# A two-block transformer kernel: the first block's layer norms, products and borders made token-major

## The chip, the cores and the metric

The kernel runs on one core of one Trainium2 chip. The metric is the device time of one execution in microseconds (us), the median of several. TensorE (PE) does the matrix products, VectorE (DVE), ScalarE (ACT) and GpSimd (POOL) the rest, and SyncE (SP) issues the weight loads.

## The reference, cut to what matters

Input `x` is 256 tokens of 1024 channels, float32. A first block of two layers and then a second block of two layers are computed. One layer of the first block is:

```python
y = _even_mixer(h, ...) if i == 0 else _odd_mixer(h, ...)        # both end in: @ w_out
h = _layer_norm(DN_ALPHA * h + y, ln1_g[i], ln1_b[i])
u = jnp.square(jax.nn.relu(h @ mlp_w1[i])) @ mlp_w2[i]           # 1024 -> 4096 -> 1024
h = _layer_norm(DN_ALPHA * h + u, ln2_g[i], ln2_b[i])
h = h + jax.nn.sigmoid(h @ ple_gate_w[i]) * (p[i] @ ple_w[i])    # p: 256 tokens x 256
```

`_layer_norm` takes mean and variance over the 1024 channels of a token. One layer of the second block is a gated feed-forward (1024 to 2816 and back), a mixer, and another gated feed-forward, with rms norms around each.

## The kernel before

All weights stream from HBM in units of 128 x 1024 floats (512 KB) through a ring of 12 slots. SP loads unit `n + 12` as soon as TensorE has handed slot `n` back (`k.freed`, a count, in order; the loop at lines 2587 to 2590). A unit is 8 blocks of 128 x 128. A float32 product of TensorE is recorded as two instructions, so a unit that is the stationary operand against all 256 tokens is 16 instructions of 256 columns.

**First block, feature-major.** An activation lies as 8 tiles of 128 channels x 256 tokens: `k.x` holds the residual and, after a norm, its result. `pe_columns` (L275 to L291) takes a unit as stationary blocks and the activation as the moving operand. `pe_unit` (L257 to L272) does the same for the down product. A layer norm sums over channels, which lie across partitions here, so `tail_tensor` (L2469) sums with products against a tile of ones: L2479 for the mean, L350 for the squares. `tail_vector.norm` (L2526) adds the residual (L2532), waits for the channel sums, subtracts the mean (L2537), takes the reciprocal of the deviation (L371) and scales (L2541). `tail_scalar.norm` squares (L359), takes the root (L364) and adds the bias (L2510). Each step needs the whole of the step before, and the next product needs the end of it. After the second norm come 8 units of gate product (L284 under `tail_tensor`), sigmoid (L2520), product with the embedding (L2549) and the sum with `k.x` (L2554). The embedding's 2 units are put beside the second norm (`embedded`, L2470). The output projections of both mixers are 8 units by `pe_columns` (L1869, L2289).

**Between the blocks.** `pe_square_sum` and `dve_rstd` make one feature-major rms norm. `turn_x` (L736) transposes the residual to token-major, and `turned_x` (L1132) copies it.

**Second block, token-major.** The residual `k.x_tok` is 2 tiles of 128 tokens x 1024 channels. A down or output product has 128 x 128 of the activation stationary and 512 columns of weight rows moving: 8 instructions of 512 columns for a unit (`pe_ffn_tok`, L458; `down`, L467). At a border the two token tiles are staggered. The last TAIL = 5 units are run for tile 0 first, `y_done` is counted, and they are run for tile 1 while ScalarE and VectorE norm tile 0 (`act_boundary`, L548; `dve_boundary`, L570). `pe_turn_h` (L399) transposes a normed tile into PSUM, 8 pieces of 128 x 128, and ScalarE and VectorE copy half each into `k.h`. `pe_lead` (L415) then runs the first units of the next product for tile 0 alone (128 columns an instruction, L425) and after that for tile 1 (L441), so that tile 1's norm has work beside it. The lead is LEAD = 3 hidden tiles of 2 units; the second tile's transposes stand ahead of the last unit of the first pass.

Each engine runs its own instructions in order; every `wait_ge` holds all that is behind it on that engine. The first block's mixers (`even_*`, `odd_*`) read `k.x`. Tables of sines and cosines for the odd mixer are made by `tables_vector` and `tables_scalar` (L2439, L2461) after the even mixer, on VectorE and ScalarE.

## Time and profile before

| | |
|---|---|
| median of 3 runs | 2330.22 us (2330.14 to 2334.64) |
| the profiled execution | 2334.19 us, its span 2332.3 us |
| TensorE busy | 2225.5 us, 95% |
| VectorE, ScalarE, GpSimd busy | 492.4, 342.0, 101.4 us |
| mean granted TensorE clock | 0.956 |
| HBM read | 296.98 MB, 128 GB/s over the span |
| chain that ended last | PE 92%, DVE 5%, ACT 1%, issue 1%, DVEq 1% |

The chain is followed back from the last instruction: what is on it sets the time. Busy time of an engine overlaps that of the others, and matmul ends are modelled, so two starts are a better measure of TensorE's work than its busy time. The granted clock is a share of full speed (2.4 GHz), and a stretch at 0.5 is 1.2 GHz.

### The profile page before, as it was taken

How to read it: one execution, taken by the hardware profiler on the slowest of the kernel's cores; microseconds unless marked ns; L12 is line 12 of the kernel's file. 1: busy time of each engine (PE TensorE's matmuls, PEld its weight loads, DVE VectorE, ACT ScalarE, POOL GpSimd, SP SyncE). 2: the span in 40 equal slices, each digit the busy share in tenths (PEclk: the TensorE clock that was granted, in tenths of full speed). 3: DMA queues.
4: the chain of work that ended last, by engine and by line, in shares of the span. 5: the costliest groups of instructions: out<-in, count | busy, mean ns of one | idle time of the engine just before them, and what ended most of it. 6: DMA issues, size and time to landing. Idle time of an engine off the chain costs nothing.

```text
span 2332.3 us, 26353 instructions
## 1 busy us (share of the span) xinstructions
PE 2225.5 (95%) x10308; PEld 1757.5 (75%) x10308; DVE 492.4 (21%) x1056; ACT 342.0 (15%) x773; POOL 101.4 (4%) x132
## 2 busy tenths in 40 slices
PE   8978899999878999999999999999999999999998
PEld 6755788888756788877777886877687778867776
DVE  0336310012452200021000463100110015530001
ACT  1113210001111100020000351100110013511001
POOL 0000000000000000000000070000000001600000
PEclk9965999999879999999999999999999999989999
DMA  6410244444202344434444421544464444124443
GB/s 256 149 37 0 73 145 153 153 135 134 93 35 67 114 153 153 150 130 129 151 153 143 148 71 57 178 153 153 145 218 153 153 149 140 63 68 158 153 153 117
DMA packets 81584, 299.47 MB, mean 128 GB/s; under 512 B 9120, under 2 KB 9248, under 8 KB 81248
## 3 DMA queue, kind: packets, MB, share of 16 engines
q1 hardware_dynamic: 80352, 293.87, 38.1%
q0 software_dynamic: 1152, 4.45, 0.5%
q8 instruction: 60, 0.98, 0.2%
q14 instruction: 20, 0.16, 0.0%
HBM read 296.98 MB, written 1.05 MB: 128 GB/s over the span
## 4 chain that ended last, share of the span: by engine, by line
PE 92%; DVE 5%; ACT 1%; issue 1%; DVEq 1%; DMA 0%; ACTq 0%; SPq 0%
PE psum L284 46%; PE psum L469 12%; PE psum L266 10%; PE psum L724 7%; PE psum L1674 5%; PE psum L2161 3%; PE psum L441 2%; PE psum L425 2%; PE psum L1558 1%; PE psum L2479 1%; PE psum L350 1%; PE psum L1622 1%; PE psum L404 0%; DVE sq L578 0%; DVE x L582 0%
## 5 line engine op out<-in xcount | busy, mean ns | idle before, releaser
L284 PE MATMUL psum<-h,ring 128*128 128x256 f32 x2976 | 654.7, 379 | 0.0
L284 PEld LDWEIGHTS psum<-h,ring 128*128 128x128 f32 x2976 | 565.1, 190 | 105.7 <-issue 32.5
L284 PE MATMUL psum<-x,ring 128*128 128x256 f32 x1728 | 391.4, 384 | 17.9 <-ACT x L2510 7.1
L284 PEld LDWEIGHTS psum<-x,ring 128*128 128x128 f32 x1728 | 332.8, 193 | 66.5 <-issue 16.3
L266 PE MATMUL psum<-hid,ring 128*128 128x256 f32 x1024 | 231.1, 379 | 0.0
L266 PEld LDWEIGHTS psum<-hid,ring 128*128 128x128 f32 x1024 | 194.6, 190 | 26.5
L469 PE MATMUL psum<-ring,hid 128*128 128x512 f32 x448 | 201.4, 592 | 0.0
L523 ACT ACTIVATE hid_act<-psum 128x256 f32<-128x256 f32 x88 | 33.8, 384 | 783.1 <-PE psum L284 729.0
L469 PEld LDWEIGHTS psum<-ring,hid 128*128 128x128 f32 x448 | 85.1, 190 | 83.2 <-issue 80.4
L538 DVE TENSOR_TENSOR hid<-psum,hid_act 128x256 f32<-128x256 f32 x56 | 23.8, 425 | 568.8 <-ACT hid_act L523 568.8
L469 PE MATMUL psum<-ring,space 128*128 128x512 f32 x256 | 112.3, 592 | 0.0
L339 DVE TENSOR_TENSOR hid<-psum,hid_act 128x256 f32<-128x256 f32 x64 | 27.2, 425 | 402.2 <-ACT hid_act L330 402.2
L469 PEld LDWEIGHTS psum<-ring,space 128*128 128x128 f32 x256 | 48.1, 190 | 54.5 <-issue 53.1
L330 ACT ACTIVATE hid_act<-psum 128x256 f32<-128x256 f32 x64 | 24.6, 384 | 402.8 <-PE psum L284 402.8
L1416 POOL TENSOR_TENSOR space<-space 128x256 f32<-128x256 f32 x90 | 70.5, 783 | 28.4 <-ACT space L1024 15.5
L1674 PE MATMUL psum<-space 128*64 128x128 f32 (+7 forms) x276 | 67.4, 407 | 1.9 <-DVE space L2015 1.0
L724 PE MATMUL psum<-ring,cat 128*128 128x512 f32 x128 | 66.4, 647 | 0.0
L1674 PEld LDWEIGHTS psum<-space 128*64 128x64 f32 (+3 forms) x276 | 47.6, 229 | 22.9 <-issue 13.2
L425 PEld LDWEIGHTS psum<-h,ring 128*128 128x128 f32 x512 | 60.3, 196 | 3.9 <-issue 3.4
L425 PE MATMUL psum<-h,ring 128*128 128x128 f32 x512 | 61.7, 281 | 1.3 <-DVE h L1130 1.3
L2161 PE MATMUL psum<-space 128*128 128x128 f32 (+3 forms) x224 | 46.7, 366 | 16.1 <-DVE space L2434 13.0
L441 PE MATMUL psum<-h,ring 128*128 128x128 f32 x512 | 58.2, 275 | 0.0
(328 smaller groups left out, 1620.7 us busy)
## 6 DMA issues: line engine op xcount, KB each, us to landing
ring<-in_weights SPq DMA_DIRECT2D x552, 512.0 KB, 3.3
space<-in_gains POOLq DMA_DIRECT2D x6, 512.0 KB, 4.5
const<-in_consts SPq DMA_DIRECT2D x1, 1493.0 KB, 11.0
x<-in_x SPq DMA_DIRECT2D x1, 1024.0 KB, 4.9
out<-x SPq DMA_DIRECT2D x2, 512.0 KB, 2.6
space<-in_params POOLq DMA_DIRECT2D x2, 509.5 KB, 4.5
space<-in_params SPq DMA_DIRECT2D x1, 659.0 KB, 12.0
space<-in_positions SPq DMA_DIRECT2D x1, 128.0 KB, 13.7
```

The source lines that it names most:

```text
L266: last = pe.matmul(out, unit[:, part, :], rhs, start=start, stop=stop, skip_group_check=True)
L284: last = pe.matmul(out, unit[:, i, :], rhs[:, i, :], start=(i == 0), stop=(i == KD - 1), skip_group_check=True)
L330: act.activation(k.hid_act[:, f % 2, :], k.bank(4 + f % 2)[:, 0, :], func).then_inc(k.act_ready, 1)
L339: dve.tensor_tensor(k.hid[:, f % 2, :], k.bank(4 + f % 2)[:, int(gated), :], k.hid_act[:, f % 2, :], ALU.mult).then_inc(k.hid_ready, 1)
L425: ins = pe.matmul(out[:, half(0)], unit[:, i, :], k.h[:, i, half(0)], start=(i == 0), stop=(i == KD - 1), skip_group_check=True)
L441: last = pe.matmul(out[:, half(1)], unit[:, i, :], k.h[:, i, half(1)], start=(i == 0), stop=(i == KD - 1), skip_group_check=True)
L469: last = pe.matmul(k.psum[:, 2 * tt + b, :], hidden_tile(k, s, f, tiles)[:, half(tt)], unit[:, b * 512:b * 512 + 512], start=(f == 0), sto ...
L523: act.activation(k.hid_act[:, f % 2, :], k.bank(4 + f % 2 if bank is None else bank)[:, 0, :], ACT.Silu).then_inc(k.act_ready, 1)
L724: return pe.matmul(out, lhsT, rhs, start=start, stop=stop, skip_group_check=True)
L1416: pool.tensor_tensor(s.zd[:, tile, :], s.zd[:, tile, :], s.product[:, t % PRODUCTS, :], ALU.add).then_inc(s.product_added, 1)
L1674: return pe.matmul(out, lhsT, rhs, start=start, stop=stop, skip_group_check=True)
L2161: return pe.matmul(out, lhsT, rhs, start=start, stop=stop, skip_group_check=True)
```

## The change

- The output projections, the down product, the gate and the embedding product of the first block take the activation as stationary operand and the weight rows as moving operand, by token tile (`pe_staggered_rows`, `pe_ffn_tok`). Their weights are laid out in rows. `pe_ffn_tok` serves both blocks; ungated it has a lead of 4 units.
- Layer norms are done on a tile of 128 tokens: statistics by `bn_stats` on VectorE, the root on ScalarE, subtract and scale on VectorE, transposes on TensorE, gain and bias with the copies out of PSUM.
- The residual with gain and bias is made by GpSimd (`tail_pool`) from gain and bias rows, which it loads broadcast.
- The four borders of a layer are staggered like those of the second block. The last one goes straight into the second block's first norm, and the feature-major norm and `turn_x` go.
- `x` is loaded to `k.h`, and once more token-major (1024 KB) behind the positions. `tables_vector` and `tables_scalar` run earlier in the even mixer: before the wait for `v` on VectorE, and after the `Ln` on ScalarE.
- `act_root_table` runs a one-element square root before the wait at every border, in the second block too.

```diff
-LEAD, TAIL = 3, 5
+LEAD, TAIL = {False: 4, True: 3}, 5
...
-    if n is not None:
-        pe_normed(s, pe, n, 0)
-    first(len(outs) - 1)
-    if n is not None:
-        pe_turn_h(k, s, pe, n, 1)
+    pe_normed(k, pe, n, 0)
+    first(early)
+    pe_turn_h(k, pe, n, 1, src)
     first(len(outs))
-    if n is not None:
-        pe_normed(s, pe, n, 1)
+    pe_normed(k, pe, n, 1)
...
+def pe_rows(k, pe, w, units, lhs, tt, first, last):
+    for j, unit in enumerate(units):
+        for b in range(2):
+            ins = pe.matmul(k.psum[:, 2 * tt + b, :], lhs(j)[:, half(tt)], unit[:, b * 512:b * 512 + 512],
+                            start=first and j == 0, stop=last and j == len(units) - 1, skip_group_check=True)
+            if b == 0 and tt == 0 and j == 0:
+                pe_hand_back(k, w, ins)
+            if b == 0 and tt == 1 and j > 0:
+                pe_hand_back(k, w, ins, 1)
+    return ins
+def pe_staggered_rows(k, pe, w, lhs, n, before_last):
+    units = [pe_take(k, pe, w) for _ in range(KD)]
+    pe_rows(k, pe, w, units, lhs, 0, True, True).then_inc(k.y_done, 1)
+    w.owed += KD
+    before_last(0)
+    pe_rows(k, pe, w, units[:-1], lhs, 1, True, False)
+    before_last(1)
+    for b in range(2):
+        last = pe.matmul(k.psum[:, 2 + b, :], lhs(KD - 1)[:, half(1)], units[-1][:, b * 512:b * 512 + 512],
+                         start=False, stop=True, skip_group_check=True)
+        if b == 0:
+            pe_hand_back(k, w, last, 1)
+    last.then_inc(k.y_done, 1)
...
+def hidden_bank(f, gated):
+    if f < LEAD[gated]:
+        return (4, 5, 6)[f] if gated else 4 + f
+    return 4 + f % 2
...
-    for f in range(LEAD - 1):
+    pe_lead(k, pe, w, [k.bank(hidden_bank(f, gated))[:, j, :] for f in range(lead) for j in range(ins)], n_in, early,
+            src, done)
+    for f in range(lead - 1):
         whole(f, base + f + 1)
-    w.n["hidden"] = base + LEAD
-    step(LEAD)
-    w.hidden_tiles(pe, LEAD + 1, tiles - TAIL + 1, 4, step)
+    w.n["hidden"] = base + lead
...
+        if f == tiles - 1 and turn_out:
+            pe_turn_h(k, pe, n_out, 0, k.h_tok)
...
+def act_root_table(k, act):
+    act.activation(k.spare, k.eps(RMS_EPS), ACT.Sqrt)
 def act_boundary(k, s, act, n, gain, halved):
+    act_root_table(k, act)
+    g = border(1, 0, n)
     for tt in range(2):
-        act.wait_ge(s.y_done, 2 * n + tt + 1)
...
+def out_projected(k, pe, w, n):
+    pe_staggered_rows(k, pe, w, lambda i: k.cat[:, i, :], n,
+                      lambda tt: pe_turn_h(k, pe, n, 0, k.h_tok) if tt else None)
...
-    pe.wait_ge(k.x_ready, PARTS)
-    for _ in range(8):
-        pe_columns(k, pe, w, pe_next_tile(k, pe, w), k.x).then_inc(k.proj_ready, 1)
+    pe_lead(k, pe, w, [pe_next_tile(k, pe, w) for _ in range(4)], border(0, 0, PLE), 2, k.x_tok,
+            lambda n, last: last.then_inc(k.proj_ready, 1))
+    for _ in range(4):
+        pe_columns(k, pe, w, pe_next_tile(k, pe, w), k.h).then_inc(k.proj_ready, 1)
...
+    ln1, ln2, ple = (border(0, layer, b) for b in (LN1, LN2, PLE))
+    pe_ffn_tok(k, pe, w, FF1, False, f.held, ln1, ln2, 3, k.h_tok)
+    for c in range(2):
+        unit = pe_take(k, pe, w)
+        for tt in range(2):
+            for b in range(2):
+                last = pe.matmul(k.psum[:, 4 + 2 * tt + b, :], f.embed[:, layer * 2 + c, half(tt)],
+                                 unit[:, b * 512:b * 512 + 512], start=(c == 0), stop=(c == 1), skip_group_check=True)
+                if tt + b == 0:
+                    pe_hand_back(k, w, last)
+        w.owed += 1
+    pe_turn_h(k, pe, ln2, 1, k.h_tok)
+    pe_normed(k, pe, ln2, 0)
+    def between_tiles(tt):
+        if tt == 0:
+            pe_normed(k, pe, ln2, 1)
+        else:
+            pe_turn_h(k, pe, ple, 0, k.h_tok if layer else k.x_tok)
+    pe_staggered_rows(k, pe, w, lambda i: k.h[:, i, :], ple, between_tiles)
...
+def tail_scalar(k, f, s, act, w, layer):
+    def norm(which, gain, bias):
+        n = border(0, layer, which)
+        act_root_table(k, act)
+        for tt in range(2):
+            act.wait_ge(f.ln_stats_ready, 2 * (2 * layer + which) + tt + 1)
+            act.activation(f.ln_std[:, tt:tt + 1], f.ln_stats[:, tt, 1:2], ACT.Sqrt, bias=k.eps(LN_EPS)).then_inc(
+                f.ln_std_ready, 1)
+            act.wait_ge(k.h_turned, (2 * n + tt) * 2 + 1)
+            for j in range(4):
+                last = act.activation(k.h[:, j, half(tt)], k.bank(2 * tt, P)[:, j, :], ACT.Identity,
+                                      bias=f.p(bias, layer * KD + j), scale=f.p(gain, layer * KD + j))
+            last.then_inc(k.h_low, 1)
+    norm(LN1, "ln1_g", "ln1_b")
+    act_ffn_tok(k, act, w, FF1, False)
+    norm(LN2, "ln2_g", "ln2_b")
+    n = border(0, layer, PLE)
+    def gate(tt):
+        act.wait_ge(k.y_done, 2 * n + tt + 1)
+        act.activation(f.sig[:, tt, :], k.acc_tok[:, tt, :], ACT.Sigmoid).then_inc(f.gate_ready, 1)
+    gate(0)
+    if layer == LAYERS - 1:
+        act.wait_ge(s.params, 16)
+        act.wait_ge(s.x_new, 1)
+        act_rms_gained(k, s, act, n, -1, 0, f.sig[:, 0, :], "ffn1_pre_g")
+        gate(1)
+        act.wait_ge(s.x_new, 2)
+        act_rms_gained(k, s, act, n, -1, 1, f.sig[:, 1, :], "ffn1_pre_g")
+        return
+    for tt in range(2):
+        act.wait_ge(k.h_turned, (2 * n + tt) * 2 + 1)
+        act.activation(k.h[:, 0:4, half(tt)], k.bank(2 * tt, P), ACT.Copy).then_inc(k.h_low, 1)
+        if tt == 0:
+            gate(1)
+def tail_vector(k, f, s, dve, w, layer):
+    def norm(which, gain, bias):
+        n = border(0, layer, which)
+        if which == LN2:
+            dve.wait_ge(f.residual, 2 * (2 * layer) + 2)
+        elif layer == 0:
+            dve.wait_ge(f.x_tok_loaded, 16)
+        for tt in range(2):
+            y, parts, r = k.x_tok[:, tt, :], f.ln_parts[:, 2 * tt:2 * tt + 2, :], f.ln_rstd[:, tt:tt + 1]
+            dve.wait_ge(k.y_done, 2 * n + tt + 1)
+            dve.scalar_tensor_tensor(y, y, ALPHA, k.acc_tok[:, tt, :], ALU.mult, ALU.add)
+            dve.drain()
+            for b in range(2):
+                dve.bn_stats(parts[:, b, :], y[:, b * 512:b * 512 + 512])
+            dve.drain()
+            dve.bn_aggr(f.ln_stats[:, tt, :], parts).then_inc(f.ln_stats_ready, 1)
+            dve.wait_ge(f.ln_std_ready, 2 * (2 * layer + which) + tt + 1)
+            dve.reciprocal(r, f.ln_std[:, tt:tt + 1])
+            dve.drain()
+            for b in range(2):
+                cols = slice(b * 512, b * 512 + 512)
+                dve.tensor_scalar(k.h_tok[:, tt, cols], y[:, cols], f.ln_stats[:, tt, 0:1], r, ALU.subtract,
+                                  ALU.mult).then_inc(k.h_scaled, 1)
+            dve.wait_ge(k.h_turned, (2 * n + tt) * 2 + 2)
+            for j in range(4):
+                i = layer * KD + 4 + j
+                last = dve.tensor_scalar(k.h[:, 4 + j, half(tt)], k.bank(2 * tt + 1, P)[:, j, :], f.p(gain, i),
+                                         f.p(bias, i), ALU.mult, ALU.add)
+            last.then_inc(k.h_high, 1)
+    norm(LN1, "ln1_g", "ln1_b")
+    dve_ffn_tok(k, dve, w, FF1, False, f.held)
+    norm(LN2, "ln2_g", "ln2_b")
+    n = border(0, layer, PLE)
+    dve.wait_ge(f.residual, 2 * (2 * layer + 1) + 2)
+    for tt in range(2):
+        dve.wait_ge(f.gate_ready, 2 * layer + tt + 1)
+        emb = k.psum[:, 4 + 2 * tt:6 + 2 * tt, :].rearrange("p b c -> p (b c)")
+        dve.tensor_tensor(f.sig[:, tt, :], f.sig[:, tt, :], emb, ALU.mult)
+        dve.drain()
+        if layer == LAYERS - 1:
+            dve.tensor_tensor(k.x_tok[:, tt, :], k.x_tok[:, tt, :], f.sig[:, tt, :], ALU.add).then_inc(s.x_new, 1)
+            dve_rms_gained(k, s, dve, n, -1, tt, "ffn1_pre_g")
+            continue
+        for b in range(2):
+            cols = slice(b * 512, b * 512 + 512)
+            dve.tensor_tensor(k.x_tok[:, tt, cols], k.x_tok[:, tt, cols], f.sig[:, tt, cols], ALU.add).then_inc(
+                k.h_scaled, 1)
+        dve.wait_ge(k.h_turned, (2 * n + tt) * 2 + 2)
+        dve.tensor_copy(k.h[:, 4:8, half(tt)], k.bank(2 * tt + 1, P)).then_inc(k.h_high, 1)
...
+def tail_pool(k, f, s, pool, layer, rows, params):
+    pool.wait_ge(k.y_done, 2 * border(0, layer, LN1) + 2)
+    for i in range(4):
+        pool.dma_start(f.rows4[:, i, :], rows[4 * layer + i:4 * layer + i + 1, :].broadcast_to([P, D])).then_inc(
+            f.rows_loaded[i // 2], 16)
+    if layer == LAYERS - 1:
+        pool.dma_start(s.par, params[0]).then_inc(s.params, 16)
+    for which in (LN1, LN2):
+        n = border(0, layer, which)
+        pool.wait_ge(f.rows_loaded[which], 32 * (layer + 1))
+        for tt in range(2):
+            pool.wait_ge(k.h_scaled, (2 * n + tt) * 2 + 2)
+            pool.tensor_tensor(k.x_tok[:, tt, :], k.h_tok[:, tt, :], f.rows4[:, 2 * which, :], ALU.mult)
+            pool.drain()
+            pool.tensor_tensor(k.x_tok[:, tt, :], k.x_tok[:, tt, :], f.rows4[:, 2 * which + 1, :], ALU.add).then_inc(
+                f.residual, 1)
...
+                    sp.dma_start(k.x_tok, x_tok).then_inc(f.x_tok_loaded, 16)
...
-    units += list(units_in(np.concatenate([w_out[0:512], w_out[512:][perm]], axis=0)))
+    units += list(np.concatenate([w_out[0:512], w_out[512:][perm]], axis=0).reshape(KD, P, UNIT))
...
-    gate, ple = list(units_in(v["ple_gate_w"][l])), list(square_units(v["ple_w"][l], P))
+    gate, ple = list(v["ple_gate_w"][l].reshape(KD, P, UNIT)), list(v["ple_w"][l].reshape(2, P, UNIT))
```

## Rows read from the trace of the kernel before

**Rows 1.** The page's part 1: busy time, share of span, instructions.
```profile
PE 2225.5 (95%) x10308; PEld 1757.5 (75%) x10308; DVE 492.4 (21%) x1056; ACT 342.0 (15%) x773; POOL 101.4 (4%) x132
```

**Rows 2.** Timeline, 246 to 306 us: start, duration, engine, line, operation, count, idle before.
```profile
250.64 27.89 PE L284 MATMUL psum<-cat,ring 128*128 128x256 f32 x128 [1.32 <-DVE cat L2124]
...
257.14 0.63 ACT L2463 ACTIVATE space<-tmp 128x512 f32<-128x512 f32 x1 [8.64 <-DVE tmp L2458]
...
278.57 2.48 DVE L2532 SCALAR_TENSOR_TENSOR x<-x,psum 128x512 f32<-128x512 f32 x4 [21.47 <-PE psum L284]
...
291.76 8.57 PE L284 MATMUL psum<-x,ring 128*128 128x256 f32 x32 [3.56 <-ACT x L2510]
```

**Rows 3.** Timeline, 498 to 600 us, TensorE.
```profile
507.36 7.07 PE L266 MATMUL psum<-hid,ring 128*128 128x256 f32 x32
...
529.40 27.86 PE L284 MATMUL psum<-x,ring 128*128 128x256 f32 x128
...
560.79 29.58 PE L284 MATMUL psum<-x,ring 128*128 128x256 f32 x128 [3.52 <-DVE x L2554]
```

**Rows 4.** The chain that ended last: start, duration, engine, tile, line, count.
```profile
734.62 27.91 PE psum L284 x128
...
1053.66 13.48 PE psum L425 x96
1067.14 10.72 PE psum L441 x96
1077.86 6.87 PE psum L469 x16
1084.73 6.91 PE psum L284 x32
```

**Rows 5.** Timeline, VectorE, 0 to 255 us.
```profile
64.04 0.69 DVE L1959 COPY space<-psum 128x512 f32<-128x512 f32 x1 [26.54 <-PE psum L1674]
```

**Rows 6.** Timeline, 1236 to 1312 us: a staggered border of the second block.
```profile
1277.30 1.28 ACT L554 ACT_TABLE_LOAD   x1
...
1284.56 1.09 PE L404 MATMUL psum<-const,tmp 128*128 128x128 f32 x8 [1.66 <-DVE tmp L589]
...
1285.49 1.88 PE L469 MATMUL psum<-ring,space 128*128 128x512 f32 x4
...
1294.11 1.09 PE L404 MATMUL psum<-const,tmp 128*128 128x128 f32 x8 [1.37 <-DVE tmp L589]
```

**Rows 7.** Timeline, 1895 to 1940 us: the same border, next layer.
```profile
1918.72 1.09 PE L404 MATMUL psum<-const,tmp 128*128 128x128 f32 x8 [1.28 <-DVE tmp L589]
```

**Rows 8.** Two stretches: engine busy (count), PEclk (granted clock share), DMA, GB/s.
```profile
1054.00:1060.00 6.00, 6.00 (x34) 5.51 (x33) 4.76 (x10) 0.00 (x0) 0.00 (x0) 0.72 0.00 0
...
1276.00:1298.00 22.00, 18.96 (x112) 13.64 (x111) 8.82 (x14) 9.28 (x21) 0.00 (x0) 1.00 0.38 121
```

**Rows 9.** Groups by line and shape: count | busy us, mean ns | idle before.
```profile
L578 DVE SCALAR_TENSOR_TENSOR sq<-psum,space 128x1024 f32<-128x1024 f32 x12 | 15.4, 1284 | 0.9
...
L589 DVE TENSOR_SCALAR tmp<-x,space 128x512 f32<-128x512 f32 x20 | 8.8, 483 | 0.8
...
L1160 DVE BATCH_NORM_STATS2 space<-psum 128x6 f32<-128x64 f32 x16 | 2.5, 219 | 15.0 <-PE psum L724 15.0
...
L566 ACT ACTIVATE h<-psum,space 128x128 f32<-128x128 f32 x40 | 11.4, 368 | 26.7 <-PE psum L404 26.7
...
L1247 DVE TENSOR_TENSOR space<-space 128x512 f32<-128x512 f32 x2 | 1.4, 692 | 0.1
...
L1266 DVE TENSOR_TENSOR space<-space 128x512 f32<-128x512 f32 x2 | 2.4, 1214 | 0.0
```

**Rows 10.** Groups by line and shape, GpSimd.
```profile
L1426 POOL TENSOR_TENSOR space<-space 128x512 f32<-128x512 f32 x2 | 3.4, 1712 | 0.0
```

**Rows 11.** The page's part 6: DMA issues, KB each, median us to landing.
```profile
ring<-in_weights SPq DMA_DIRECT2D x552, 512.0 KB, 3.3
```

**Rows 12.** The first fill of the ring: engine busy (count), PEclk, DMA, GB/s.
```profile
9.00:11.00 2.00, 2.00 (x6) 1.60 (x5) 0.00 (x0) 0.00 (x0) 0.00 (x0) 1.00 1.07 448
```

More of the change, by code:

```diff
@@ L23 @@
 LAYERS = 2
-PARTS = 4
 HEAD = 64
@@ L76 @@
 BOUNDARIES = 3 * LAYERS
+LN1, LN2, PLE = range(3)
 def columns(table):
@@ L345, in pe_square_sum @@
-def pe_square_sum(k, pe, w):
-    for j in range(PARTS):
-        pe.wait_ge(k.sq_ready, w.value("norm", scale=PARTS) + j + 1)
-        for i in part_tiles(j):
-            last = pe.matmul(k.bank(6)[:, 0, :], k.c("ones"), k.sq[:, i, :], start=(i == 0), stop=(i == KD - 1))
-    last.then_inc(k.sum_ready, 1)
-    w.n["norm"] += 1
-def act_squares(k, act, w, src, wait_part):
-    for j in range(PARTS):
-        wait_part(j)
-        act.activation(part(k.sq, j), part(src, j), ACT.Square).then_inc(k.sq_ready, 1)
@@ L468, in down @@
         for b in range(2):
-            last = pe.matmul(k.psum[:, 2 * tt + b, :], hidden_tile(k, s, f, tiles)[:, half(tt)],
+            last = pe.matmul(k.psum[:, 2 * tt + b, :], hidden_tile(k, held, f, tiles, gated)[:, half(tt)],
                              unit[:, b * 512:b * 512 + 512], start=(f == 0), stop=(f == tiles - 1), skip_group_check=True)
@@ L1867, in even_tensor @@
     pe.wait_ge(*f.dve.at("out"))
-    for n in range(KD):
-        last = pe_columns(k, pe, w, k.acc[:, n, :], k.cat)
-    last.then_inc(k.acc_ready, 1)
-    w.n["acc"] += 1
+    out_projected(k, pe, w, border(0, 0, LN1))
 def even_scalar(k, f, act, w):
@@ L2287, in odd_tensor @@
     pe.wait_ge(*f.oact.at("up7"))
-    for n in range(KD):
-        last = pe_columns(k, pe, w, k.acc[:, n, :], k.cat)
-    last.then_inc(k.acc_ready, 1)
-    w.n["acc"] += 1
+    out_projected(k, pe, w, border(0, 1, LN1))
 def odd_scalar(k, f, act, w):
@@ L2469, in tail_tensor @@
 def tail_tensor(k, f, pe, w, layer):
-    def embedded(j):
-        pe_unit(k, pe, w, [(k.acc[:, 4 * j + n, :], n * 2 + c, f.embed[:, layer * 2 + c, :],
-                            c == 0 and n % 2 == 0, c == 1) for n in range(4) for c in range(2)])
-    def norm(meanwhile=False):
-        for j in range(PARTS):
-            pe.wait_ge(f.y_ready, w.value("norm", scale=PARTS) + j + 1)
-            for i in part_tiles(j):
-                last = pe.matmul(k.bank(7)[:, 0, :], k.c("ones"), k.x[:, i, :], start=(i == 0), stop=(i == KD - 1))
-        last.then_inc(f.mean_ready, 1)
-        if meanwhile:
-            embedded(0)
-        pe_square_sum(k, pe, w)
-        if meanwhile:
-            embedded(1)
```

422 lines of the change are left out of this document (123 added, 299 removed).

## The prediction

> **What bounds the kernel now.** The page's busy line comes first: TensorE is busy for 95% of the span, VectorE for 21% [rows 1]. The time is TensorE's work plus the holes in it. The chain of waits and the timeline then show where the holes are. In the first block they stand at each border, where the whole of a norm lies between two products. The reader is to see three things there.
>
> Before the first feed-forward of layer 0 the product ends where VectorE starts at 278.57, and the next begins at 291.76: 13.2 us with only the small channel sums in them. Its first 32 instructions then take until 300.3, 8.57 us, for which the chain shows 6.91 later [rows 2, 4]: 1.7 us of low clock. Before the gate product the down product ends at 507.36 + 7.07 = 514.4 and the gate starts at 529.40. Of these 15.0 us, 6.9 are the embedding's work. The next mixer starts 3.5 us after the gate and needs 29.58 for what takes 27.6 elsewhere [rows 3]. Between the blocks, behind the feature-major norm, 96 instructions take 13.48 us and the next 96 of the same shape 10.72 [rows 4]; the granted clock of the slow ones is 0.72, a mix of both levels, 1.2 and 2.4 GHz [rows 8].
>
> The second block already has the new form of border. Its holes are one of 1.66 and one of 1.37 us [rows 6], and the clock through them is 1.00 [rows 8]. So the trace holds the price list for the new first block.
>
> **Unit prices.** At full clock a unit against 256 tokens is 6.91 / 2 = 3.455 us, a unit in rows (8 of the 16 instructions in 6.87) 3.435, a half pass of a lead (16 of 96 instructions in 10.72) 1.787, all from the chain [rows 4]. Eight transposes take 1285.49 - 1284.56 = 0.93 from start to start where they follow a hole [rows 6]; the following price of a series without a hole is a little less, and I take 0.9.
>
> **Layer 0, from its output product to the odd mixer.**
> - Output product in rows, 8 units: 27.5. Transposes of tile 0: 0.9.
> - Lead of 4 units in two half passes: 8 x 1.787 = 14.3. Transposes of tile 1: 0.9.
> - The other 28 units into the hidden layer: 96.7. Down product, 32 units: 109.9.
> - Transposes of tile 0, second norm: 0.9. Embedding, 2 units: 6.9. Transposes of tile 1: 0.9.
> - Gate, 8 units: 27.5. Transposes of tile 0: 0.9.
>
> The sum is 287.3. Before, the stretch is 560.79 - 250.64 = 310.15 [rows 2, 3]. It saves 22.9. The mixer's first 8 units are then 14.3 + 0.9 + 4 x 3.455 = 29.0, with 0.1 of wait below, for 29.58: 0.5.
>
> **Layer 1.** The same 287.3 stands for 1053.66 - 734.62 = 319.0: 31.7 saved, since this stretch also holds the feature-major norm, its 16 slow sum products and `turn_x`. The second block's lead is then 12 half passes, 21.4, 0.9 of transposes and 0.6 of wait (below), together 22.9, for 13.48 + 10.72 = 24.2: 1.3.
>
> **Is each norm hidden?** Of the tile that is normed first, yes: it has 7 units of tile 1 beside it (12.0 us), or 4 (6.9). The chain of the second tile decides. From its `y_done` to the first half scaled: sum with the residual 1.28; two `bn_stats`; `bn_aggr`; root; reciprocal; scale 0.48. `bn_stats` of 512 elements is not in the trace; of 64 it takes 0.22 [rows 9]. Below it is bounded by a plain pass over 512 (0.48), above by 8 times the row, 1.75. VectorE's other passes grow by about 1 ns an element, so I take 0.69, near a two-input pass of 512 [rows 9]. `bn_aggr`, root and reciprocal I estimate at 0.9 with their hand-overs. That is 4.2 (3.7 to 6.3).
> - First norm: the cover is 3 half passes, 5.4. No wait at 4.2; 0.9 at the upper end, twice.
> - After the transposes one half pass (1.8) covers the copies into `k.h`: four of ScalarE at 0.37 at most [rows 9] beside four of VectorE. No wait; 0.3 if VectorE's were 0.5 each.
> - Second norm: the cover is the embedding, 6.9. No wait.
> - Gate of layer 0: sigmoid of 1024 about 1.0, product 1.28, first half of the sum 0.69, hand-overs 0.5: 3.5 against 3.6 of cover, and the second half 0.7 later: 0.1.
> - Gate of layer 1: ScalarE must finish tile 0's rms copies, then load the sigmoid's table (1.28, as its row [rows 6]) and comes to tile 1 about 0.3 late. Sigmoid 1.0, product 1.3, sum 1.3, square 1.25, table 1.28, root, reciprocal, scale and hand-overs 1.3: 7.7 against 4 half passes, 7.15: 0.6 (0 to 2.5 if all but the table take 30% longer).
>
> **The preloaded root table in the second block.** At each border after a gated product the table load stands inside tile 0's chain, 1.28 [rows 6], and TensorE waits at the end of that chain: 1.66 at the first border of this kind and 1.28 at the last [rows 6, 7], three in all. The load moves ahead of `y_done`, where ScalarE idles. 3 x 1.28 = 3.8 saved. The one ahead of the output is on tile 0 alone and gives nothing. *ScalarE: Activation LUTs* of the Trainium skill (section "What ACT_TABLE_LOAD costs") adds a drain of about 1.38 us to every switch. The row shows 1.28 and the next instruction right behind it; with the drain the whole holes would go, 4.2 instead of 3.8.
>
> **What is put beside other work and costed at nothing.**
> - Sine tables: before, VectorE's part lay inside the output product and ScalarE waited 8.64 for it [rows 2]. Now it lies in a stretch in which VectorE idles for 26.5 us [rows 5]. Without that cover it would be some 8.
> - The second load of `x`, 1 MB ahead of unit 4 in SP's queue: at 448 GB/s [rows 12] some 2.3 us; unit 4 is needed 4 units after the start (over 13.8 us). I see cover; uncovered it would be 2.3, once.
> - GpSimd's residual: per tile two passes of 1024, 2 x 3.4 by its row for 512 [rows 10]; four tiles a layer. It is needed by the next sum with the residual, which is over 20 us off after the second norm and 200 after the first. The broadcast rows (2 MB on GpSimd's queue) are asked for at the end of the output product and needed by GpSimd alone.
> - The ring: 8 units are held through a staggered product and come back one by one in its second pass, 1.7 us apart. Four more are loaded already, 14.3 us of lead. A load lands in 3.3 us [rows 11]. No wait.
>
> A rule speaks against GpSimd's part. The rows: a VectorE pass over 512 with two SBUF inputs takes 0.69 in one place and 1.21 in another, beside the convolution [rows 9]. The *GPSIMD Engine Reference* of the Trainium skill (section "Key points") says that GpSimd shares its SBUF interfaces with VectorE. By that rule tile 1's second norm, which runs beside GpSimd's pass over tile 0, would grow, and the trace agrees that such growth exists. By the rows' ratio, 1.75, a chain of 4.2 becomes 6.6 at most, still under the 6.9 of cover. At the first norm GpSimd still waits for its rows. So the sum is the same by either.
>
> **The sum.** 22.9 + 0.5 + 31.7 + 1.3 + 3.8 = 60.2. Profiled execution: 2334.19 - 60.2 = 2274.0 (span 2332.3, 1.9 around it). The median of the runs shown is 4.0 lower than the profiled execution, so the forecast against it is 2330.2 - 60.2 = **2270**.
>
> **Rivals.**
> 1. *The second tile's chain does not fit.* If it takes twice what I take, 8.4, the first norms wait 3.0 each, the second ones 1.5 each, the gate of layer 0 3.6 and that of layer 1 7: 20 us, time 2290; half of it, 2280. For it: the chain has five hand-overs, and two prices are estimates. Against it: the rms chain of the second block is longer, has a cover of about the same size and waits 1.37 [rows 6]. Chance 0.10.
> 2. *The ring runs dry.* If the 8 returned units were loaded one at a time, 3.3 each, 26.4, against 14.3 of work in the ring, each of four staggered products is followed by 12 of wait: 48 us, time 2318. Against it: the first fill moves 448 GB/s, a unit in 1.2 us [rows 12]. Chance 0.04.
> 3. *The clock falls at the new borders* (the side slower than before). The stretches with short waits and narrow instructions, output and gate product with their leads, are 4 x 42 = 168 us at 2.4 GHz. At 1.2 GHz they would cost 168 more: 2438. It decides from 60 us, a bit over a third of them. For it: the clock did fall after today's holes. Against it: those are 3.5 us and longer, and the second block's staggered border is at 1.00 throughout [rows 8]. Chance 0.02.
> 4. *The form alone does nothing and only the borders count* is inside the forecast: rows against columns give 100 x 0.02 = 2 us of the 60.
>
> **How the numbers follow.** Forecast 0.84, with a range of its own of 2264 to 2277 (upper ends of the waits and the second load of `x` +7, transposes and hand-overs -3, spread of runs). Range 2263 to 2284 with half of rival 1. What this kernel can tell from no change is about 0.2%, 4.7 us. Faster: forecast, rivals 1 and 2, 0.97; same 0.01; slower 0.02.
>
> **What would show it.** TensorE's timeline: `pe_turn_h` for tile 1 with under 0.3 us idle before it in the first block, 0.6 ahead of the second; 287 us from output product to next mixer, twice; clock 1.00 at all borders there; the 1.66 hole down to 0.4. It is wrong if holes of over 1 us stand before the transposes, if TensorE waits for the ring behind a staggered product, or if the mixers grow.

## The result, and the profile after

The changed kernel takes 2262.4 us in the median (2257.5 to 2267.0, four runs) against 2330.2 for the kernel before: ratio 0.971, 95% interval 0.969 to 0.973. The forecast was 2270 and its range began at 2263, so it is missed by 0.6 us on the fast side. Two more comparisons (below) gave 2274.8 and 2268.8, both inside the range; over all 14 runs of the changed kernel the median is 2268.6, over 73 of the kernel before 2330.4, a gain of 61.7.

The page of after, part 1 (engine, busy us, share of the span, instructions), answers to [rows 1]: TensorE is busy for 51 us less and stands idle for 25 us less. Busy time counts instructions at a low clock in full, so the 51 us are not only fewer instructions.

```profile
PE 2174.6 (96%) x9634; PEld 1577.1 (70%) x9634; DVE 489.9 (22%) x1059; ACT 336.7 (15%) x772; POOL 137.2 (6%) x156
```

TensorE's timeline of after at the first norm of layer 0 (start, us, engine, line, operation, count, idle before) answers to [rows 2]:

```profile
270.61 1.04 PE L290 MATMUL psum<-const,tmp 128*128 128x128 f32 x8
271.49 1.88 PE L351 MATMUL psum<-ring,cat 128*128 128x512 f32 x4
273.20 5.55 PE L309 MATMUL psum<-h,ring 128*128 128x128 f32 x48
278.59 1.04 PE L290 MATMUL psum<-const,tmp 128*128 128x128 f32 x8
279.46 1.95 PE L309 MATMUL psum<-h,ring 128*128 128x128 f32 x16
281.25 7.31 PE L322 MATMUL psum<-h,ring 128*128 128x128 f32 x64
```

No row has an idle time, where before 13.2 us lay open. The chain of tile 1 behind it is on VectorE's timeline:

```profile
273.41 1.22 DVE L2429 SCALAR_TENSOR_TENSOR x<-x,psum 128x1024 f32<-128x1024 f32 x1 [0.35 <-PE psum L351]
274.70 1.29 DVE L2432 BATCH_NORM_STATS2 space<-x 128x6 f32<-128x512 f32 x2
276.06 0.21 DVE L2434 BATCH_NORM_AGGREGATE space<-space 128x2 f32<-128x12 f32 x1
276.63 0.16 DVE L2436 RECIPROCAL space<-space 128x1 f32<-128x1 f32 x1 [0.36 <-ACT space L2388]
276.88 1.00 DVE L2440 TENSOR_SCALAR tmp<-x,space 128x512 f32<-128x512 f32 x2
```

Its first half is scaled at 277.4, 4.0 us after the start; TensorE asks for it at 278.6.

The gate of layer 0 and the odd mixer's lead answer to [rows 3], the second block's lead and the first border behind a gated product to [rows 4, 6]:

```profile
529.33 1.04 PE L290 MATMUL psum<-const,x 128*128 128x128 f32 x8
530.20 1.88 PE L351 MATMUL psum<-ring,h 128*128 128x512 f32 x4
531.92 3.73 PE L309 MATMUL psum<-h,ring 128*128 128x128 f32 x32
535.49 1.04 PE L290 MATMUL psum<-const,x 128*128 128x128 f32 x8
...
986.35 7.31 PE L309 MATMUL psum<-h,ring 128*128 128x128 f32 x64
994.06 1.09 PE L290 MATMUL psum<-const,tmp 128*128 128x128 f32 x8 [0.41 <-DVE tmp L521]
...
1214.44 1.09 PE L290 MATMUL psum<-const,tmp 128*128 128x128 f32 x8
```

The hole of 0.41 is the wait forecast at 0.6; the one of 1.66 in the second block is gone. So far the sum holds. It has no term for the mixers, and they moved too. The starts of the output products and of the leads behind them cut every profile into parts. "Stretch" is from output product to next mixer, "FFN" the first three feed-forward stretches of the second block, each from lead to mixer or next lead; all in us; a1, a2 and b1 are runs told of below:

```
profiled execution   to 1st output  stretch 0  odd mixer  stretch 1  FFN                  second mixers
before                      250.64     310.15     173.83     319.04  233.55 231.76 231.55  170.85 174.23
before, again (b1)          251.48     310.42     166.91     319.40  232.18 231.77 231.54  172.69 170.90
after                       244.76     287.16     167.26     287.17  230.74 230.43 230.21  170.94 170.93
after, again (a1)           245.71     287.16     170.23     287.17  230.74 230.43 230.21  174.26 174.25
after, again (a2)           251.47     287.17     169.51     287.16  230.75 230.42 230.21  172.65 176.63
```

The changed kernel's stretches repeat to 0.02 us. The mixers, whose code is nearly the same in all five (the even one has the sine tables at its head, the odd one another lead), move by up to 6.7 (even), 6.9 (odd) and 5.8 us (second).

### The profile page after: what moved, and what is told of

It reads as the page before. It is cut to its first block, busy times and chain, and to the rows that moved or that the text cites. A ratio compares the mean times of both kernels' runs of the same rounds, so it can differ in the third digit from the quotient of the medians.

```text
span 2256.3 us, 24984 instructions
## 1 busy us (share of the span) xinstructions
PE 2174.6 (96%) x9634; PEld 1577.1 (70%) x9634; DVE 489.9 (22%) x1059; ACT 336.7 (15%) x772; POOL 137.2 (6%) x156
## 3 DMA queue, kind: packets, MB, share of 16 engines
HBM read 302.22 MB, written 1.05 MB: 134 GB/s over the span
## 4 chain that ended last, share of the span: by engine, by line
PE 93%; DVE 4%; ACT 1%; issue 1%; DVEq 1%; DMA 0%; ACTq 0%; SPq 0%
PE psum L249 41%; PE psum L381 23%; PE psum L648 6%; PE psum L1566 5%; PE psum L333 5%; PE psum L322 3%; PE psum L309 3%; PE psum L2051 3%; PE psum L1444 1%; PE psum L290 1%; PE psum L2366 1%; PE psum L1508 1%; DVE space L1914 0%; DMA ring<-in_weights 0%; DVE space L2322 0%
## 5 line engine op out<-in xcount | busy, mean ns | idle before, releaser
L249 PE MATMUL psum<-h,ring 128*128 128x256 f32 x4256 | 941.3, 379 | 7.0 <-DMA ring<-in_weights 7.0
L249 PEld LDWEIGHTS psum<-h,ring 128*128 128x128 f32 x4256 | 809.2, 190 | 167.8 <-issue 63.9
L381 PE MATMUL psum<-ring,hid 128*128 128x512 f32 x816 | 366.8, 592 | 0.0
L381 PEld LDWEIGHTS psum<-ring,hid 128*128 128x128 f32 x816 | 155.0, 190 | 151.6 <-issue 146.4
L381 PE MATMUL psum<-ring,space 128*128 128x512 f32 x400 | 175.4, 592 | 0.0
L309 PEld LDWEIGHTS psum<-h,ring 128*128 128x128 f32 x704 | 80.5, 192 | 4.1 <-issue 2.9
L309 PE MATMUL psum<-h,ring 128*128 128x128 f32 x704 | 81.7, 275 | 0.0
L322 PE MATMUL psum<-h,ring 128*128 128x128 f32 x704 | 80.1, 275 | 0.0
L322 PEld LDWEIGHTS psum<-h,ring 128*128 128x128 f32 x704 | 79.3, 192 | 0.0
L1300 POOL TENSOR_TENSOR space<-space 128x256 f32<-128x256 f32 x90 | 70.0, 778 | 29.4 <-ACT space L928 16.6
L648 PE MATMUL psum<-ring,cat 128*128 128x512 f32 x128 | 65.1, 636 | 0.0
L333 PE MATMUL psum<-ring,cat 128*128 128x512 f32 x120 | 52.0, 594 | 1.8 <-DVE cat L2014 1.3
L1444 PE MATMUL psum<-space,ring 128*128 128x256 f32 x160 | 41.1, 413 | 12.1 <-DVE space L1461 7.0
L333 PE MATMUL psum<-ring,h 128*128 128x512 f32 x120 | 51.8, 592 | 0.0
L2051 PEld LDWEIGHTS psum<-space 128*128 128x128 f32 (+1 forms) x224 | 34.3, 220 | 25.1 <-ACT space L1527 14.2
```

Of the source, the lines that this page charges most:

```text
L249: last = pe.matmul(out, unit[:, i, :], rhs[:, i, :], start=(i == 0), stop=(i == KD - 1), skip_group_check=True)
L309: ins = pe.matmul(out[:, half(0)], unit[:, i, :], k.h[:, i, half(0)], start=(i == 0), stop=(i == KD - 1), skip_group_check=True)
L322: last = pe.matmul(out[:, half(1)], unit[:, i, :], k.h[:, i, half(1)], start=(i == 0), stop=(i == KD - 1), skip_group_check=True)
L333: ins = pe.matmul(k.psum[:, 2 * tt + b, :], lhs(j)[:, half(tt)], unit[:, b * 512:b * 512 + 512], start=first and j == 0, stop=last and j = ...
L381: last = pe.matmul(k.psum[:, 2 * tt + b, :], hidden_tile(k, held, f, tiles, gated)[:, half(tt)], unit[:, b * 512:b * 512 + 512], start=(f ...
L648: return pe.matmul(out, lhsT, rhs, start=start, stop=stop, skip_group_check=True)
```

## The experiments

**The changed kernel again** (a1, then a2). No edit.

> The changed kernel once more, unaltered. Its four runs fell into two pairs, 2257.5 and 2258.1, 2266.7 and 2267.0, and its gain was 67.8 in the medians, 76.0 in the profiled pair, where the sum gave 60.2. Theory A (the rest is TensorE's granted clock inside the mixers, which falls and rises at another place from one execution to the next): between 2257 and 2268 again; the stretches from output product to next mixer stay at 287.3 and 287.2 us; the mixers of the first block (244.8 and 167.1 in the profile of after) differ from those by some us with no code changed, and time and mean clock go together. Rival B (the change itself shortens the mixers): mixers within 1 us of 244.8 and 167.1 again.

2274.8 us (2268.2 to 2275.0). The upper end of the expectation was too low by 7, and the gain is 57.3 by this comparison. The stretches are the same and the mixers are not (table): theory A holds, rival B falls. Where the time is can be seen in TensorE's windows (us busy, instructions, granted clock, DMA share, GB/s) over the end of the last mixer, after first, this run second:

```profile
1986.70:2006.70 20.00, 19.18 (x113) 0.83 0.00 1
2006.70:2019.70 13.00, 13.00 (x39) 1.00 0.71 228
```
```profile
1993.90:2013.90 20.00, 20.00 (x105) 0.59 0.00 0
2013.90:2026.90 13.00, 13.00 (x38) 0.98 0.48 158
```

The clock is below full in both, for longer in the second: 3.3 us.

> The changed kernel, a third comparison with the kernel before. Theory A: the stretches from output product to next mixer 287.2 twice, even mixer 245 or 251, odd one 167 to 170, second ones 170.9, 172.8 or 174.3; the gain between 55 and 70, so that the three comparisons lie around the sum of 60.2.

2268.8 us (2268.5 to 2274.4), 61.5 less than before on that chip. In this run the even mixer's attention is at 0.50 to 245 us, and the mixer takes 251.5, as in the old kernel: so the changed kernel doesn't always have the shorter time. The second of its second mixers, 176.6, is longer than any expected.

**The old kernel again** (b1).

> The kernel before, unaltered. Chance of the clock alone: the even mixer somewhere between 244 and 252 us to its output product, the odd one between 167 and 174. If the even mixer's 5 to 6 us belong to the code: 250.6 to 251.7 again.

2329.8 (2321.9 to 2334.3), ratio 1.000 (0.998 to 1.001). Odd mixer 166.9, the changed kernel's time: the 6.6 us that it seemed to have gained were chance of the first profile. TensorE's granted clock over the odd mixer is 0.92 here and in after, 0.85 in the first profile of before. Even mixer 251.5, which is what was expected if its time belonged to the code; it takes the changed kernel's own 251.5 above to speak against that.

**The x of the first products later.** The first load of `x` behind three ring units.

```diff
-            sp.dma_start(k.h, x).then_inc(k.x_loaded, 16)
+                if slot == 2:
+                    sp.dma_start(k.h, x).then_inc(k.x_loaded, 16)
```

> The changed kernel with the first load of x put behind three ring units in SP's queue, so that all of TensorE's work starts some 3 to 4 us later; nothing else differs. Theory A (clock levels inside the mixers depend on chance): 2262.4 + 3.5 = 2266 with the same spread of about 10 us between runs, and a mixer that differs by some us from the 167.1 of after. Rival B (the mixers are shorter for a reason in the code): 3.5 us more than after, all of it at the start, mixers as in after.

2265.5 (2261.0 to 2279.5). TensorE starts 2.3 us later, the first output product 8.8 later, for the attention's clock rises later; the second mixers are at 170.9 twice. Delay and time don't go together: the spread of 18 us is larger than the delay, as theory A had it.

**The sine tables alone**, in the old kernel: `tables_vector` and `tables_scalar` where the changed kernel has them.

> The kernel before with the sine tables' work of VectorE and ScalarE moved to where the changed kernel has it, at the head of the even mixer, and nothing else. If that edit made the even mixer shorter (by where TensorE's waits and so its clock fall): 245 instead of 251 to the output product, and the 8.6 us wait of ScalarE in the output product gone at no gain, 2324 to 2326. If it is chance: the same distribution as before.

2328.1 (2322.8 to 2332.4), ratio 0.999 (0.997 to 1.001): no difference that can be measured. Even mixer 253.2, so the edit doesn't shorten it. Stretch 0 is 308.7 for 310.4: behind the same hole of 3.56 us the first 32 instructions take 7.14 us here, 8.57 and 8.83 in the two profiles of before. What a low clock costs behind a hole varies too.

**The root table alone**, in the old kernel, and all but it in the new one.

```diff
 def act_boundary(k, s, act, n, gain, halved):
+    act.activation(k.spare, k.eps(RMS_EPS), ACT.Sqrt)
```

> The kernel before with one line of the change: the square root's table is loaded ahead of the product's end at each border of the second block. Both theories: the three holes of 1.66, 1.37 and 1.28 us after gated products fall to about 0.4, so 3.8 us less than before in the second block's stretches. By the page's drain of 1.38 us with a table switch it would be 4.2. Theory A adds that the mixers may differ from those of before by some us either way although nothing in front of them changed, so the time is 2326.4, plus or minus 5; rival B says 2326.4 within 1, since the first block is the old one.

2322.7 (2312.5 to 2330.3), ratio 0.996 (0.995 to 0.998). The FFN stretches are 230.83, 230.43 and 230.20, for 232.18, 231.77 and 231.54 in the old kernel's second profile: 1.35, 1.34 and 1.34, 4.0 in all. The median is 9.5 us under that of before on the same chip, more than the 3.8 within 1 of rival B.

> The changed kernel without the table load ahead of the product's end in the second block's borders (in the first block it stays). Both: the load stands again inside tile 0's chain, holes of 1.66, 1.37 and 1.28 for about 0.4 each, so 3.8 us over after in the feed-forward stretches (each stretch of 230.4 and 230.2 becomes 231.8 and 231.6). Theory A: the time itself moves by 3.8 plus or minus 5, with mixers that change by themselves. Rival B: 3.8 within 1.

2271.0 (2263.2 to 2275.7); the stretches are 232.08, 231.77 and 231.54, 4.0 more again, from the other side. The sum had 3.8. The other 5.5 of the 9.5 us by which the median of the run before this one moved are in no stretch.

**Without the stagger** in the first block: form in rows kept, both tiles awaited ahead of each lead.

```diff
     pe_normed(k, pe, n, 0)
-    first(early)
-    pe_turn_h(k, pe, n, 1, src)
-    first(len(outs))
-    pe_normed(k, pe, n, 1)
+    pe_turn_h(k, pe, n, 1, src)
+    pe_normed(k, pe, n, 1)
+    first(len(outs))
```

> The changed kernel with the first block's leads unstaggered: both tiles' norms are waited for, and tile 1 is turned, before the first half pass. It puts a hole ahead of each lead and leaves the form in rows. Both: at each first norm the chain of tile 1 (4.0 us to the first half scaled in after, 0.5 for the second, 0.9 of transposes, 1.3 of copies) stands free, 6.1 more, twice; at the gate of layer 0 5.3, at that of layer 1 9.5 more: 27 us over after, 2289. The other norms (second norms, with the embedding as cover) stay. Theory B, in which the missing hole ahead of the odd mixer gave it the 6.7 us: odd mixer back to about 173.8 behind its hole, 2296. Theory A: the odd mixer anywhere between 167 and 174 plus its hole of 5.

2304.0 (2296.7 to 2305.0), 29.1 over the changed kernel of the same chip and 28.1 under the old one. So of the 57.3 us of that chip about half go with the stagger. Stretches 302.2 and 306.1: with the second block's first stretch (232.23 for 230.74) 35.4 more. TensorE's timeline of this kernel at the first norm and at the gate of layer 1:

```profile
278.29 1.94 PE L290 MATMUL psum<-const,tmp 128*128 128x128 f32 x8 [4.19 <-DVE tmp L2445]
281.74 9.94 PE L309 MATMUL psum<-h,ring 128*128 128x128 f32 x64 [1.51 <-ACT h L2397]
...
1018.92 1.94 PE L290 MATMUL psum<-const,tmp 128*128 128x128 f32 x8 [7.64 <-DVE tmp L526]
1021.69 13.87 PE L309 MATMUL psum<-h,ring 128*128 128x128 f32 x96 [0.83 <-ACT h L496]
```

The holes (4.2 + 1.5, 3.2 + 0.8, 4.2 + 1.5, 7.6 + 0.8) sum to 23.9; the other 11.5 are slow instructions behind them: eight transposes in 1.94 for 1.04, the 64 instructions of 4 half passes in 9.94 for 7.3, with the clock at 0.50 from 278 to 282 us and 0.74 in the ten us after. That term was missing in the expectation of 27. The odd mixer, behind a hole of 4 us, takes 168.0 in this profile, within the 166.9 to 173.8 of the table: a hole ahead of it doesn't lengthen it.

**A longer chain.** `bn_stats` of tile 1 three more times in each half.

> The changed kernel with bn_stats of tile 1 run four times over in each half (six more at 0.65 us and a drain each, about 4.2 us in the chain of the second tile's norm, four norms). It measures the slack that the stagger leaves. By the profile of after, tile 1 at the first norm has 1.2 us of slack and at the second 2.7: waits before its transposes of about 3.0, 1.5, 3.0 and 1.5, 9 us in all over after, if the clock does not fall in them. If the slack were in fact the 0 to 0.3 that a chain of the upper bound would leave, all 17 us.

2291.2 (2279.6 to 2293.0). TensorE's timeline at the norms of layer 0:

```profile
288.77 1.40 PE L290 MATMUL psum<-const,tmp 128*128 128x128 f32 x8 [3.33 <-DVE tmp L2443]
...
516.97 1.11 PE L290 MATMUL psum<-const,tmp 128*128 128x128 f32 x8 [2.22 <-DVE tmp L2443]
```

In layer 1 they are 3.32 and 1.84. The chain is 4.6 longer (5.9 for 1.3 in `bn_stats`), so the slack of the change is 1.3 us at the first norms and 2.4 to 2.8 at the second. The holes are 10.7, the stretches grow by 9.5 + 7.4 = 16.9: again over half as much on top at a low clock (0.58 from 289 to 292 us). The median, 22.6 over that of all runs of the changed kernel, would by itself have spoken for the 17 us of the rival and so for a slack near zero; the holes in the trace show that it isn't.

**Holding the clock up.** In all profiles of both kernels the even mixer's attention runs at 0.50, 1.2 GHz, from 190 us on, with no idle time. It leaves that level at about 228 (after, a1), at 240 (before) or at 245 (a2), and the mixer takes 245 or 251 us. If the level hangs on what TensorE is given to do, other products among the attention's own must move it. First a product of two constants, 128x128 by 512, into the score bank that the real scores then overwrite.

```diff
+        mm(k.psum[:, u % 4, :], k.c("ones"), k.c("head4"))
         mm(att.scores(u, tt)[:, 0, :], q, f.ks[...
```

> The changed kernel with one more product per unit of the even mixer's attention: a full 128x128 by 512 product of two constants into the score bank, which the real scores then overwrite. In the profiles of before and after the granted clock is 0.50 from 190 to 225 us although TensorE has no idle time there, with products of 64 rows and 64 or 128 columns, and rises at 240 in one and at 228 in the other. If a full-width product among them makes the clock rise (theory A extended: the level follows what runs, not only whether TensorE is busy), the 16 units at 3.4 us each fall towards 2.2: about 45 us of 0.50 become 25 with 16 x 0.21 us added, so 10 to 15 us less than after, and the same time in every run. If the clock depends on something else, 16 x 0.43 = 7 us more.

2267.4 (2264.8 to 2276.5), the median of all runs of the changed kernel within 1.2; mixer 247.1. But the clock is up from 201 us on; the product costs 1.05 at full clock, not the 0.21 that I had put down for it, since in float32 it is two instructions of 0.53. What the clock gives it takes.

> As the run with one product per unit, and besides the holes ahead of and in the first units (4.1, 3.4 and 2.2 us of waits for VectorE) are filled with 10, 8 and 5 such products. If the clock can be brought up, it is up when the attention becomes TensorE's own at 190, another 3 us or so less than with one product per unit. If not, the fill is in waits and costs at most the 2 us by which 23 products at 0.43 exceed them.

2270.1 (2268.3 to 2270.7). The clock is 1.00 from 180 us on, but the fills took TensorE 11.4, 7.0 and 4.6 us where the waits had been 4.1, 3.4 and 2.2, and the mixer takes 254.7.

The same constants read as bf16 take 0.27 or less.

```diff
+def pe_keep_up(k, pe, bank, times):
+    for _ in range(times):
+        pe.matmul(k.psum[:, bank, :], k.c("ones").bitcast(BF16)[:, 0:P], k.c("head4").bitcast(BF16)[:, 0:512],
+                  start=True, stop=True, skip_group_check=True)
```

> The full product ahead of each unit of the even mixer's attention had cost 1.05 us at full clock, since in float32 it is two instructions, and gave back what it gained. Here it is one product of the same constants read as bf16, 128x128 by 512, one per unit, overwritten as before. If it does the same for the clock, the units fall from 3.4 and 4.2 us to about 2.4 and 3.5 once the clock has risen: 5 to 10 us less than after in this mixer. If a single one does not raise the clock, 16 x 0.43 = 7 us more and 0.50 until 228 or later.

Run k1, 2270.8 (2270.7 to 2279.5): one per unit does not raise it earlier, 0.50 to 245 us, mixer 256.7.

> Two such products per unit, ten ahead of the last wait before the attention (a hole of 4.1 us) and six and four in the units that wait for VectorE. If the level follows what runs, the clock is 1.00 from 180 to 245 and the mixer ends near 233 to 236 instead of 245: 9 to 12 us less than after, and the same in all runs. The odd and the second mixers still vary by themselves (3.4 us each), so the time spreads by some 7 us. Rival: the clock stays at 0.50, 6 us more.

Run k2, 2251.9 (2251.2 to 2259.0), ratio to the kernel before 0.967 (0.965 to 0.968). Mixer 238.8, 3 us over what was expected.

> The same, and the two holes at 139 and 146 us (3.35 and 3.49) filled with 8 and 10 such products, so that the 64 products of 30 columns that follow (13.9 us at 0.50) and the four of 512 behind them run at 1.00 if the level follows what runs: some 6 to 8 us less than with the attention alone, 15 to 20 less than after. If the level does not hold there, the same as with the attention alone.

Run k3, 2249.2 (2247.1 to 2257.1), ratio 0.9645 (0.9632 to 0.9658), mixer 232.4; the 64 products of 30 columns still take 12.4 us at a low clock. TensorE's windows over the attention, of before and of this kernel:

```profile
190.00:210.00 20.00, 20.00 (x67) 0.50 0.01 1
210.00:230.00 20.00, 20.00 (x63) 0.50 0.00 0
230.00:240.00 10.00, 10.00 (x35) 0.50 0.00 0
```
```profile
190.00:210.00 20.00, 18.62 (x98) 1.00 0.00 0
210.00:230.00 20.00, 19.02 (x114) 1.00 0.01 1
230.00:240.00 10.00, 8.68 (x27) 1.00 0.17 54
```

More instructions, and idle time where there was none.

> The kernel before with the bf16 products that hold the clock up in the even mixer (as in the run k3_keep_all). With the clock pinned there in both kernels, the mixer takes the same: about 232.5 to 238 in both. Then the difference between this kernel and k3_keep_all is the stretches' and the odd and second mixers': 2249.2 + 60 = 2309, plus or minus 5. If the even mixer's difference had belonged to the change, it would still be 5 us longer here.

Run b3, 2315.9 (2312.8 to 2320.6), 2 us above the 2309 plus 5. The even mixer of the old kernel is now 232.3, that of the changed one 232.4: with the clock held, the change doesn't touch it. The two kernels with the clock held are 66.7 us apart, and 60.8 by the next run of the changed one below (2255.1), on other chips; the sum of the prediction was 60.2.

> The changed kernel with bf16 products of constants in the even mixer as in k3_keep_all, three more behind each eight of the 64 products of 30 columns, and in the odd mixer ten ahead of its attention and two in each of its units. If the level follows what runs: the 12.4 us of the 64 products at 0.50 fall to 9 with the added ones included, the odd mixer from 168-171 to about 164, together some 7 us less than k3_keep_all: 2243. If the added products only take TensorE's time there: 2 to 5 us more than k3_keep_all.

Run k4, 2260.2 (2257.4 to 2266.8), 11 us over k3 where the rival had 2 to 5. Even mixer 237.2, odd one 176.8. Products in every unit of the odd attention don't hold the clock: from 650 to 690 us it is 0.83 here, in after 1.00 and 0.91 over the like 40 us (from 654).

> The kernel that holds the clock up in the even mixer, on the same chip as the changed kernel: even mixer 232.4, 12 to 19 us less than the changed kernel in the medians.

Run k5, 2255.1 (2248.0 to 2259.5) beside 2268.8 for the changed kernel. Even mixer 234.4, where the same code had 232.4 in k3: with the clock held it still moves by 2 us. Odd mixer 171.7.

> As k5_keep_all_again, and in the odd mixer ten bf16 products into the wait ahead of its attention and two in each of the first three units. In k4_keep_more, with two in all units, the first 12 us of the attention ran at 1.00, but from the fifth unit on each pair took 9.9 us for the 7.4 of after, so the odd mixer took 176.8. Without them there: 165 to 167 for 168 to 171, some 3 us less than k5_keep_all_again. If the fall of the clock is only moved to the units behind, the same time.

Run k6, 2247.5 (2246.9 to 2251.2), ratio 0.9646 (0.9633 to 0.9659), which is that of k3: 21 us under the changed kernel on the same chip, and with a spread of 4 us in five runs. Odd mixer 167.4 for the 171.7 of k5 beside it; but after had 167.3 and the old kernel 166.9 without such products, so a gain of the odd mixer isn't shown by its time. The first 20 us of its attention, in after and, with the products ahead of it, in this kernel:

```profile
634.00:654.00 20.00, 17.99 (x65) 0.66 0.00 1
```
```profile
620.00:640.00 20.00, 16.60 (x80) 0.93 0.02 4
```

From the last product ahead of the attention (it starts at 618.75 in this kernel) to the end of the first hole of 2.0 us in it pass 18.0 us, for 22.3 in k5 and in after. From there to the output product pass 50.0 us, as in k5; in after 47.0.

## Why the prediction was right in its terms and wrong in its range

Measured terms are differences of the table, the old kernel by both of its profiles.

- *Layer 0, 22.9.* 310.15 - 287.16 = 23.0, and 23.3 by the second. The price list taken from the second block gave 287.3 for the new stretch; it is 287.16 in each profile with the stagger and the chain as they are.
- *Layer 1, 31.7.* 31.9, and 32.2. With the same 287.17.
- *Odd mixer's first units, 0.5; second block's lead, 1.3.* From the first of the eight units to the product behind them it was 29.4 before and is 29.0, 0.4. The lead fell from 24.2 to 23.1, 1.1, and its whole stretch by 1.5 more than the root table gives. In b1 the old lead was at a better clock and that 1.5 is 0.1: the term was itself a size that changes between executions.
- *Root tables, 3.8.* 4.0, three holes. *ScalarE: Activation LUTs* of the Trainium skill ("What ACT_TABLE_LOAD costs") has about 1.38 of drain on top of each switch; the row of the table load with the next instruction right behind it, and 1.34 gained for each, don't show it.
- *The waits of the norms.* The chain of tile 1 was taken at 4.2 and is 4.0, with `bn_stats` at 0.65 for 0.69 and both halves scaled in 1.00. No wait at the first and second norms, 0.41 for 0.6 ahead of the second block, none for 0.1 ahead of the odd mixer. Rival 1 is out, with 1.3 us of slack where it would have decided. A chain of its 8.4 would have waited: the lengthened one, 8.6, waited 3.3 where the rival had 3.0.
- *The ring.* A load ended only TensorE's first wait, 7.0 us at the start (7.1 before): rival 2 is out.
- *GpSimd.* Two passes of 1024 take 2.00 each, where 3.4 stood. It cost nothing, as forecast. The growth to 6.6 that the prediction allowed for in tile 1's second norm was not put to the test: GpSimd's passes over tile 0 ended at 495.4 us, VectorE's chain of tile 1 began at 496.0 and had its 4.0 us.
- *Rival 3, the clock at the new borders.* It doesn't fall while they are closed. The two kernels with holes there show its small form: holes of 23.9 and 10.7 us in all cost 35.4 and 16.9, half as much again. So part of the 60 us is that the old holes took their low clock with them, and this part was in the rows of the old stretches from the start.

Rival 4 was not tested by itself: the kernel without the stagger keeps the form, but has the new norms too.

These sum to 60 to 61, and the gain in the medians over all runs is 61.7. The step that failed is a term put at nothing: the prediction's sum has no term for the mixers beyond the 0.5 of the odd one's first units, as if a median of few runs held their time still, and its range leaves 3 us for "spread of runs" (from 2270 - 3 for transposes and hand-overs to 2264; the stated range begins 1 lower). The profiled execution of before had the odd mixer at its slow end (173.8), that of after had all mixers at their fast ends, and of the 76.0 us between the two executions 15.7 are the mixers', of which 0.5 was forecast. Between profiles of one and the same kernel the second mixers move by 3.4 to 5.7 us each, the odd one by 3 to 7 and the even one by up to 6.7. The three medians of the changed kernel are 2262.4, 2268.8 and 2274.8, up to 6.2 from the median of all its runs. With these 6.2 in place of the 3 below 2267 and added above 2277, the range would have been 2261 to 2283. That the first median fell outside the stated range and the two others inside is chance as far as these runs show, and so is the side on which it fell.

Open: what decides at which time the clock leaves 0.50 in the even mixer. Four of the six profiles of changed kernels that start at the same time have it early (245), none of four of old ones; that is too few to call the odds the same or different. That the sine tables alone don't bring the shorter time was shown (253.2), and with the clock held the mixer takes the same in both kernels (232.3; 232.4 and 234.4), so its work is the same.

## What to carry to other kernels

A second part of a kernel that already has the form that a first part is to get is its price list: count the units, take the durations at full clock, and the new stretch comes out to 0.2 us in 287, as far as its holes are closed. Before a term of a few us is claimed or a range is drawn, look for stretches at a granted clock between 0.50 and 1.00 or at a steady 0.50 with no idle time: they are where executions differ, and a gain of several us in a part that the change doesn't touch is to be suspected first. A stretch that is TensorE's own at 0.50 deserves the same attention as a hole: 66 cheap products that hold the clock up gave 14 to 19 us here (k5 and k3 against the median of all runs of the changed kernel). More of them, 108, gave it back in part (2260.2).

## What was unexpected of the hardware

- An engine that is busy throughout can stay at 1.2 GHz: the even mixer's attention did for 38 us in one profile and 55 in another, with products of 64 rows by 128 and 256 columns and small transposes. One bf16 product of 128x128 by 512 per unit changed nothing, two per unit, ten ahead of the stretch and six and four in two of its units held it at 2.4 GHz from 195 us on; which of these it needs was not separated. *TensorE: Matmul & The Clock Gate* of the Trainium skill ("Part 1: The HAM clock gate") calls the lower level that of an idle engine and the upper one that of a busy one; by the profile's busy time this stretch shows the lower one at 100% busy, so the profile's busy share doesn't tell which state comes.
- The second mixers take about 170.9, 172.7, 174.3 or 176.5 us in nearly all profiles (once 173.4), few values rather than a spread, with the same instructions. Why is open.
- Of a product 128x128 by 512, float32 took two instructions of 0.53 us in that stretch and bf16 one of about 0.27, both at full clock. In the down product the float32 instruction of this shape takes 0.43 from start to start.
